# One layer of a streaming step on one core: where the search part transposes a tile's picks, and where the mixers run the next unit's head

## The reference

```python
u = rmsnorm(h, g_mix);  z = u @ w_in
zq, zf, zi, zg, zx, zy = split(z)
# A: four heads, in chunks of 64 tokens; f = lb + (1 - lb) * sigmoid(zf), k = 1 - f, q = silu(zq)
S_t = diag(f_t) S_{t-1} + k_t^T i_t ;  o_t = S_t^T q_t
oA = rmsnorm(o) * silu(zg)
# B: width-4 causal conv of zx, two block-diagonal gates r and i, then a scan
a = exp(-8 * r * softplus(-lam));  b = sqrt(1 - a^2) * (i * xc);  h_t = a_t h_{t-1} + b_t
oB = h * gelu(zy)
h += concat(oA, oB) @ w_out
h += peer(rmsnorm(h, g_ffn))
h += (p @ w_ple) * sigmoid(rmsnorm(h, g_ple) @ w_ple_gate);  y = rmsnorm(h, g_final)

def peer(x):                      # 8 heads, top 16 of 128 x 128 experts, 16384 in all
    q = x @ w_q;  s = q . keys    # two halves a head
    pick the 16 best sums of the two halves' top 16;  g = softmax(those sums)
    return sum_k g_k * gelu(U[e_k] . x) * V[e_k]
```

## Time and profile before

| | us |
|---|---|
| median of 3 runs | 3629.16 (3627.43 to 3629.78) |
| the profiled execution | 3632.48, its span 3630.8 |
| mixers | from about 350 to 610 |
| search part, six rounds over the tiles | from about 1140 to 1612 |
| TensorE busy | 3233.1, 89% of the span |
| VectorE busy | 2724.1, 75% |
| ScalarE busy | 1060.8, 29% |
| GpSimd busy | 975.9, 27% |
| mean granted TensorE clock | 0.941 of full speed |

### The profile page before, as it was taken

How to read it: one execution, slowest core, us unless ns; L and a number is a source line. 1 busy time by engine, 2 the same in 40 slices (tenths; PEclk the granted TensorE clock), 3 DMA queues, 4 the chain that set the end, 5 groups by cost and what they waited for, 6 DMA issues and landing times. The chain is left out here.

```text
span 3630.8 us, 52472 instructions
## 1 busy us (share of the span) xinstructions
PE 3233.1 (89%) x17880; PEld 2942.6 (81%) x17880; DVE 2724.1 (75%) x4967; ACT 1060.8 (29%) x1419; POOL 975.9 (27%) x796
## 2 busy tenths in 40 slices
PE   6998566979979999899999987779999999999988
PEld 6998344779979988899999987768888888888778
DVE  3000766268889888889999987659999999999853
ACT  3112434121122222225555531122222222222233
POOL 0000000000002444444444446423333333333300
PEclk9999666989989999999999999889999999999989
DMA  3223221011145888889999999889999999999721
GB/s 112 86 86 108 79 76 61 18 28 39 26 125 181 253 263 252 246 252 306 323 326 324 323 332 338 298 292 352 359 352 354 359 353 350 351 357 345 248 76 53
DMA packets 411350, 822.83 MB, mean 227 GB/s; under 512 B 40704, under 2 KB 262800, under 8 KB 403856
## 3 DMA queue, kind: packets, MB, share of 16 engines
q1 hardware_dynamic: 300688, 419.27, 35.4%
q0 software_dynamic: 110592, 402.70, 32.6%
HBM read 696.74 MB, written 125.12 MB: 226 GB/s over the span
## 5 line engine op out<-in xcount | busy, mean ns | idle before, releaser
L232 PE MATMUL ea_pa<-rest_hi,ea_uhi 128*128 128x384 f32 x2048 | 711.5, 347 | 131.5 <-DVE ea_ulo L1415 129.8
L1137 POOL DMA_INDIRECT h<-in_peer_u,ga_rows x384 | 562.6, 1465 | 741.6 <-DVE ea_acc L1542 513.1
L233 PE MATMUL ea_pa<-rest_lo,ea_uhi 128*128 128x384 f32 x2048 | 698.3, 341 | 0.0
L234 PE MATMUL ea_pa<-rest_hi,ea_ulo 128*128 128x384 f32 x2048 | 698.2, 341 | 0.0
L1137 POOL DMA_INDIRECT eo_ring<-in_peer_v,ga_rows x384 | 406.3, 1058 | 695.7 <-DVE h L1826 629.1
L232 PEld LDWEIGHTS ea_pa<-rest_hi,ea_uhi 128*128 128x128 f32 x2048 | 395.5, 193 | 143.8 <-issue 93.1
L1826 DVE SCALAR_TENSOR_TENSOR h<-eo_ring,eo_share,h 128x1024 f32<-128x1024 f32 x384 | 490.9, 1279 | 0.5 <-DMA eo_ring<-in_peer_v,ga_rows 0.5
L1542 DVE CUSTOM_DVE_ANT_0 h<-h,plain 128x1024 f32<-128x1024 f32 x384 | 454.2, 1218 | 42.0 <-DMA h<-in_peer_u,ga_rows 41.9
L233 PEld LDWEIGHTS ea_pa<-rest_lo,ea_uhi 128*128 128x128 f32 x2048 | 395.6, 193 | 0.0
L234 PEld LDWEIGHTS ea_pa<-rest_hi,ea_ulo 128*128 128x128 f32 x2048 | 394.8, 193 | 0.0
L1762 ACT ACTIVATE eo_phi<-eo_prod 128x512 fp32r<-128x512 f32 x192 | 121.6, 633 | 775.7 <-DVE eo_prod L1800 724.2
(11 more groups left out here) (317 smaller groups left out, 6203.5 us busy)
## 6 DMA issues: line engine op xcount, KB each, us to landing
ea_raw<-in_peer_u SPq DMA_DIRECT2D x512, 128.0 KB, 5.7
region<-in_peer_v SPq DMA_DIRECT2D x128, 512.0 KB, 10.4
act_scratch<-ea_stage SPq DMA_DIRECT2D x128, 384.0 KB, 4.9
w_scratch<-region SPq DMA_DIRECT2D x24, 2048.0 KB, 12.0
region<-w_scratch SPq DMA_DIRECT2D x16, 1536.0 KB
region<-act_scratch SPq DMA_DIRECT2D x16, 1536.0 KB
eo_wt<-w_scratch SPq DMA_DIRECT2D x16, 1536.0 KB, 13.7
eo_at<-act_scratch SPq DMA_DIRECT2D x16, 1536.0 KB, 18.0
```

The source lines that it names most:

```text
L232: nc.tensor.matmul(out, w[0], x[0], start=first, stop=False)
L233: nc.tensor.matmul(out, w[0], x[1], start=False, stop=False)
L234: return nc.tensor.matmul(out, w[1], x[0], start=False, stop=last)
L1137: nc.gpsimd.indirect_dma_start(out=dst, out_offset=None, in_=table, in_offset=bass.IndirectOffsetOnAxis(ap=self.rows[:, m % GT, m // GT:m ...
```

## The change

In the search part TensorE's three transposes of a tile's picks stand behind the fifth of the eight blocks instead of the eighth, and ScalarE's three copies of them stand in its seventh step, behind that step's `hi`, instead of behind the eighth. VectorE's queue is as before.

In the mixers the loops are written out. The head of a unit (VectorE: L671 to L695; ScalarE: the three sigmoids and Ln; TensorE: the transpose of the state rows) stands ahead of the tail of the unit before: on VectorE behind the copies that signal `oc_ready`, on ScalarE behind Sqrt (L650) and ahead of Square, on TensorE behind the chunk products of the samples. For that q, x, the conv result and the parameters have two buffers, q and x are loaded two units ahead (the second unit's at the start), the old rows are copied out of PSUM first, Square writes to r and Gelu to ig, and a few semaphores are new. The diff, cut to its core:

```diff
@@ mixers: the loads at the start, on SP
                 for load in (load_f, load_x, load_v, load_q, load_g, load_s, load_y):
                     load(e, 0)
+                load_x(e, 1)
+                load_q(e, 1)
@@ mixers: SP, in a unit
                         e.wait_ge(o_sum, i + 1)
-                        load_q(e, i + 1)
+                        if i + 2 < 4:
+                            load_q(e, i + 2)
                         load_s(e, i + 1)
                         e.wait_ge(oc_ready, i + 1)
-                        load_x(e, i + 1)
+                        if i + 2 < 4:
+                            load_x(e, i + 2)
@@ mixers: ScalarE
-                with e.Fori(0, 4) as i:
-                    e.wait_ge(all_used, i + 1)
+                def head(i):
                     e.wait_ge(in_f, (i + 1) * 16)
+                    if i > 0:
+                        e.wait_ge(sf_used, i)
                     f(sf[:], zf[:], ACT.Sigmoid).then_inc(sig_f, 1)
...
+                    e.wait_ge(f_ready, i + 1)
+                    f(cum[:], sf[:], ACT.Ln).then_inc(ln_f, 1)
+
+                head(0)
+                for i in range(4):
+                    cur = cur_two[:, i % 2]
                     e.wait_ge(v_t, i + 1)
                     f(vtok[:], ps_v, ACT.Copy).then_inc(v_tok, 1)
-                    e.wait_ge(f_ready, i + 1)
-                    f(cum[:], sf[:], ACT.Ln).then_inc(ln_f, 1)
                     e.wait_ge(cum_ready, i + 1)
...
                     f(sf[:], sf[:], ACT.Sqrt).then_inc(sqrt_b, 1)
+                    if i + 1 < 4:
+                        head(i + 1)
                     e.wait_ge(o_sum, i + 1)
-                    f(cum[:].rearrange("p (t c) -> p t c", c=128), ps_o, ACT.Square).then_inc(o_sq, 1)
+                    e.wait_ge(oc_ready, i + 1)
+                    f(r[:].rearrange("p (t c) -> p t c", c=128), ps_o, ACT.Square).then_inc(o_sq, 1)
                     e.wait_ge(ms_ready, i + 1)
                     f(rs[:], rs[:], ACT.Sqrt).then_inc(rms_root, 1)
                     e.wait_ge(in_y, (i + 1) * 16)
-                    f(sq[:], zy[:], ACT.Gelu_apprx_tanh).then_inc(gelu_y, 1)
+                    f(ig[:], zy[:], ACT.Gelu_apprx_tanh).then_inc(gelu_y, 1)
@@ mixers: VectorE
                     e.wait_ge(state_t, i + 1)
-                    e.wait_ge(in_x, (i + 1) * 32)
-                    link(v.tensor_copy(xs[:, :, 0:3], ps_state[:, 0:24].rearrange("p (b j) -> p b j", j=3)))
+                    e.wait_ge(in_x[i % 2], (i // 2 + 1) * 32)
+                    v.tensor_copy(old[:, i % 2], ps_state[:, 0:32]).then_inc(old_ready, 1)
+                    e.wait_ge(old_ready, i + 1)
+                    link(v.tensor_copy(xs[:, :, 0:3], old[:, i % 2, 0:24].rearrange("p (b j) -> p b j", j=3)))
...
+                head(0)
+                for i in range(4):
+                    main(i)
+                    if i + 1 < 4:
+                        head(i + 1)
+                    tail(i)
@@ mixers: TensorE
-                with e.Fori(0, 4) as i:
+                def state_rows(i):
+                    e.wait_ge(in_rows, (i + 1) * 32)
+                    e.wait_ge(all_used, max(i, 1))
+                    tr(ps_state, rows_in[:], P.ident[:]).then_inc(state_t, 1)
+
+                state_rows(0)
+                for i in range(4):
                     e.wait_ge(all_used, i + 1)
-                    e.wait_ge(in_rows, (i + 1) * 32)
-                    tr(ps_state, rows_in[:], P.ident[:]).then_inc(state_t, 1)
                     e.wait_ge(in_v, (i + 1) * 16)
...
                     last.then_inc(dss_ready, 1)
+                    if i + 1 < 4:
+                        state_rows(i + 1)
                     e.wait_ge(st_ready, i + 1)
...
                     e.wait_ge(oc_ready, i + 1)
+                    e.wait_ge(old_ready, min(i + 2, 4))
                     tr(ps_rows, cols_out[:], P.ident[:]).then_inc(oc_t, 1)
@@ experts: ScalarE  (T_STEP = 4)
                     quad(i * Q_DENSE + GT, lambda r: exponentials(i + GT) if r == 2 else None)
-                    quad(i * Q_DENSE + (GT + 1))
-                    e.wait_ge(rows_t, i + 1)
-                    cols = bass.ds(i * 128, 128)
-                    for x, scale in ((0, 1.0), (1, 1.0), (2, G_SCALE)):
-                        nc.scalar.activation(picks[:, x, cols], pr[:, x], ACT.Copy, scale=scale).then_inc(picks_hi, 1)
+                    quad(i * Q_DENSE + (GT + 1), lambda r: copy_picks(i) if r == T_STEP + 2 - 4 else None)
@@ experts: TensorE
-                    quad(i * Q_DENSE + GT)
-                    quad(i * Q_DENSE + (GT + 1))
-                    e.wait_ge(rows_ready, i + 1)
-                    for n in range(3):
-                        last = nc.tensor.transpose(pr[:, n], rows[:, n], P.ident[:])
-                    last.then_inc(rows_t, 1)
+                    for r in range(4 * Q_DENSE):
+                        for n in range(ND_N):
+                            product(*at_block(i * Q_DENSE + GT, r + 1), n)
+                        if r == T_STEP:
+                            e.wait_ge(rows_ready, i + 1)
+                            for x in range(3):
+                                last = nc.tensor.transpose(pr[:, x], rows[:, x], P.ident[:])
+                            last.then_inc(rows_t, 1)
```

More of the change, by code:

```diff
@@ L564, in mixers @@
          st_ready, sn_ready, att_sum, att_ready, qdz_ready, o_sum, o_sq, ms_ready, rms_root, on_ready, on_t,
-         state_t, xc_ready, silu_g, gates, va_ready, sqrt_b, gelu_y, oc_ready, oc_t, rows_ready, self_ok) = (s(n) for n in (
+         state_t, old_ready, sf_used, e3_used, xc_ready, silu_g, gates, va_ready, sqrt_b, gelu_y, oc_ready, oc_t, rows_ready, self_ok) = (s(n) for n in (
              "stored", "cur", "used", "sig_f", "sig_q", "sig_g", "sig_r", "sig_i", "f", "ln_f", "cum", "dl",
@@ L568, in mixers @@
              "st", "sn", "att_sum", "att", "qdz", "o_sum", "o_sq", "ms", "rms_root", "on", "on_t",
-             "state_t", "xc", "silu_g", "gates", "va", "sqrt_b", "gelu_y", "oc", "oc_t", "rows", "self"))
+             "state_t", "old", "sf_used", "e3_used", "xc", "silu_g", "gates", "va", "sqrt_b", "gelu_y", "oc", "oc_t", "rows", "self"))
         NSTORE = 6
@@ L612, in _ @@
                 load_wg(e, 0)
-                with e.Fori(0, 3) as i:
-                    unit(i, True)
-                unit(3, False)
+                for i in range(4):
+                    unit(i, i < 3)
                 e.wait_ge(stored, 5 * NSTORE * 16)
@@ L697, in _, with main @@
                     e.wait_ge(xc_ready, i + 1)
+                def main(i):
+                    zq, xc, xp, xs, cur = (x[:, i % 2] for x in (zq_two, xc_two, xp_two, xs_two, cur_two))
                     e.wait_ge(ln_f, i + 1)
@@ L770, in _, with tail @@
                     v.tensor_copy(cols_out[:, 28:36], by(xc[:, SAMPLE], DS)[:, :, DS - 1]).then_inc(oc_ready, 1)
+                def tail(i):
+                    zq, xc, xp, xs, cur = (x[:, i % 2] for x in (zq_two, xc_two, xp_two, xs_two, cur_two))
                     e.wait_ge(o_sq, i + 1)
-                    link(v.tensor_reduce(rs[:], cum[:].rearrange("p (t c) -> p t c", c=128), AX.X, ALU.add))
+                    link(v.tensor_reduce(rs[:], r[:].rearrange("p (t c) -> p t c", c=128), AX.X, ALU.add))
                     v.tensor_scalar(rs[:], rs[:], 1.0 / 128, EPS, ALU.mult, ALU.add).then_inc(ms_ready, 1)
@@ L793, in _ @@
                 mm, tr = nc.tensor.matmul, nc.tensor.transpose
-                with e.Fori(0, 4) as i:
+                def state_rows(i):
[3 more added lines that the diff above has]
+                state_rows(0)
+                for i in range(4):
+                    zq, xc = zq_two[:, i % 2], xc_two[:, i % 2]
                     e.wait_ge(all_used, i + 1)
-                    e.wait_ge(in_rows, (i + 1) * 32)
-                    tr(ps_state, rows_in[:], P.ident[:]).then_inc(state_t, 1)
                     e.wait_ge(in_v, (i + 1) * 16)
@@ L1367, in exponentials, with copy_picks @@
                     nc.scalar.activation(rows[:, 2], rows[:, 2], ACT.Exp).then_inc(exped, 1)
+                def copy_picks(i):
+                    e.wait_ge(rows_t, i + 1)
+                    cols = bass.ds(i * 128, 128)
+                    for x, scale in ((0, 1.0), (1, 1.0), (2, G_SCALE)):
+                        nc.scalar.activation(picks[:, x, cols], pr[:, x], ACT.Copy, scale=scale).then_inc(picks_hi, 1)
                 hi(0, 0)
```

82 lines of the change are left out of this document (45 added, 37 removed).

## The result

The changed kernel takes 3548.27 us (3545.12 to 3549.67) beside 3628.81 for the kernel before: a ratio of 0.9777, 95% interval 0.976 to 0.9794. Run again later, it was 3553.32 beside 3626.43, ratio 0.9802 (0.9785 to 0.9818). So 80.5 and 73.1 us less; forecast were 75.9. The profiled execution took 3547.42 us; the one of before, 3632.48, lay above its median, so the two traces differ by 85.1.

What follows compares the result with a forecast made beforehand. VectorE's waits were taken to bound the search part (last step on the picks) and the mixers (norm's sum, then the next head). Savings of 54.3 + 21.6 = 75.9 us gave a median of 3553 us, range 3541 to 3580.

Steps and rivals of the forecast that it cites:

- Middle boundaries: Dense search part, between tiles: VectorE's first five waits at the last step on the picks vanish, giving back 44.8 us.
- Last boundary: End of the dense search part, no following tile: 9.5 us back, between TensorE's 8.3 and VectorE's 13.67.
- Gathers at no cost: Dense search part: the same gathered bytes in less time, 285 GB/s at DMA share 0.95, costing nothing.
- Rival 4: Dense search part: VectorE waits for gathered rows, costing 157 us, total 3710 us; chance 4%.
- The head fits: Mixers: the next unit's head, 8.6 us on VectorE, fits the 8.64 to 9.4 us gap between scan and norm.
- Rival 2: Mixers: the moved head makes Square late and the norm slips, losing the 24.9 us gain, total 3578 us; chance 6%.
- The added table load is covered: Mixers, before the norm's root: ScalarE's extra 1.28 us load fits in its 1.63 us idle stretch, costing nothing.
- The mixers' pace: Mixers: moving the head three times saves 8.3 us each, 24.9 us in all, bounds 24.9 and 27.6.
- Up to attention: Mixers, from the turn of the units: attention products start at 11.7 us instead of 19.98, 8.3 us a unit.
- later than 12 us: Mixers: attention starting more than 12 us after the turn of the units would show the forecast wrong.
- nothing changes: Mixers, behind the start of attention: the rest of each unit takes as long as before, no gain or loss.
- The start: Start of the mixers: three added loads, 1.18 MB at 354 GB/s, delay the first state rows by 3.3 us.

Runs made afterwards that it cites:

- the two runs with all fillers: Changed kernel, state rows ahead of most loads, identity transposes ahead of v's transposes, gates, attention and output products: 3529.57 us; with q, g also ahead of rows: 3526.43 us.

## Why the prediction was right, point by point

**Middle boundaries: right.** Five were to give back 44.8 us. From the first turn to the sixth, before took 393.23 us (1147.17 to 1540.40) and the changed kernel 347.88 (1119.97 to 1467.85): 45.35. The rounds take 69.4 to 70.0 us (69.6). The slack of the copies is 7.9 us (7), and the run one block later shows what it hangs on. VectorE bounds, as the working had it. TensorE's wait for the softmax cost nothing that shows.

**Last boundary: the reason right, the size 2.6 us too large.** I took 9.5 us, between TensorE's 8.3 and VectorE's 13.67. The dense part became shorter by 55.7 in the mean of the table's rows with and without the search change, so 10.4 fall to this boundary; the weighted part became 3.5 longer. In its first pair of copies, 45.1 us apart instead of 43.6, VectorE now waits for the split behind TensorE's blocks, as the rows at 1540.70 and 1552.04 show. Over the whole weighted part these waits are 4.3 us in the first trace of the changed kernel, 1.2 in the second and 3.6 in the search part alone, where it is 5.8, 2.4 and 4.0 us longer than 501.1: most of it. Two of the later ones in the first trace (1815.80 and 1904.36) come behind waits of ScalarE for a store of the weights (6.0 us until 1810.69, 6.7 until 1899.27); the second trace has no such later wait of VectorE. Net 6.9, below my lower end of 8.3: I had not counted what VectorE loses behind the boundary. The search part as a whole gives 52.2 by the traces (54.3 predicted, bounds 49.8 and 58.5) and 55.9 by the medians of the run with it alone.

**Gathers at no cost: right.** 286 GB/s at 0.94 stand where 285 and 0.95 were worked out, and VectorE waits 0.5 us for gathered rows in the dense part. Rival 4 did not come.

**The head fits: right.** The norm's sum waits 0.24 and 0.31 us behind the moved head in the second and third units and nothing in the first. Rival 2 did not come.

**The added table load is covered: right.** It runs from 472.12 to 473.40 while VectorE sums, and the root starts at 473.80, when VectorE's L800 has ended. The Trainium skill (ScalarE: Activation LUTs, What ACT_TABLE_LOAD costs) adds a drain of some 1380 ns to a load. By that rule the trace disagrees here too: the load starts as Square ends, and the root starts 0.40 us after the load's end.

**The mixers' pace: two steps mis-sized, in opposite directions.** I worked out 24.9 us, with an upper bound of 27.6. From the first scan to the output projection it was 241.8 us in the mean of the three traces with the old mixers and 213.0 in the five with the new: 28.8, above the bound. The units came 50.2 to 51.7 us apart, two of fifteen 53.5; some 53 was expected of all. The means of the pieces say where.

*Up to attention: less than worked out.* I had attention 11.7 us after the turn of the units, and "later than 12 us" was named as a sign of being wrong. The sign came: 12.0, 12.5 and 12.7 us in the first trace, 13.1 three times in the second. The step that failed is the 1.38 us from the gates to attention. I had ScalarE's table load done at 9.4, ahead of the gates' end; but ScalarE stands at the wait for the gates first and loads behind it (438.61), so it is 2.76 us in every moved unit. Where the gates took less than the 6.85 of the earlier trace rows, as the 5.64 above, that hid a part of it. Up to attention 22.4 us came back, not 24.9.

*From attention on: "nothing changes" was wrong by 6.4 us.* The attention products themselves are 3.5 us shorter over four units, by TensorE's clock: in units two to four of the five traces 13 of 15 took 2.25 us, in the old mixers one of nine. I had taken their row from the earlier trace rows at 0.50 and left it there. The other 2.9 us lie behind them: the norm's sum comes 1.0 us sooner behind the last of the four small copies, the tail is 1.3 shorter, and 0.6 lies between attention and those copies. The runs don't explain these three.

Why the level was mostly the upper one is open too. The changed kernel's shorter pauses (2.76 instead of 3.70 us ahead of attention, 1.31 instead of 7.05 ahead of the gates) go with it, but units with the same pauses came out differently, and with pauses of 1.4 to 2.0 us, in the two runs with all fillers, two of six still had 3.9 us.

**The start: about right in size, not quite in its reason.** 3.3 us were worked out from 1.18 MB at 354 GB/s. The rows came 3.3 us later and the first scan 3.4 to 4.9. The run with the loads moved back recovers all of it. But the trace of the changed kernel has the rows themselves issued later, at 362.45 instead of 358.57, since SP issues the three loads from 358.02 to 361.99 and the next block starts behind them. From issue to the transposes the rows took 6.8 us, before 7.4. So the delay is one of issuing, and the bytes give nearly the same figure. Before, then after:

```profile
358.57 0.38 SPq L517 DMA_DIRECT2D mx_rows_in<-in_state_conv  x1
```

```profile
359.12 2.87 SPq L493 DMA_DIRECT2D mx_zq<-z_scratch  x1
362.45 0.38 SPq L520 DMA_DIRECT2D mx_rows_in<-in_state_conv  x1
```

Whether this long issue of 2.87 us is itself a wait for the bytes ahead isn't shown. They do count: with only f and x ahead, the rows took 1.9 us from issue to the transposes (358.11 to 360.04).

**The sum: in part luck.** 52.2 from the search part and 28.8 − 3.8 from the mixers (3.8 is how much later the first scan came, in the mean of the same traces) make 77.2, between the two medians' 73.1 and 80.5. The errors (search part 2 less, mixers 3.4 more, and within the mixers 2.5 less and 6.4 more) lie on opposite sides, so the total came out nearer than its terms. The 85.1 of the two profiled executions contain 7 us of spread.

## What to carry to other kernels

A wait that ends at another engine's queue is moved by moving the work ahead in that queue, and the check is a table of when each block ends on each engine: it gave the slack of 7 us here, and one block later the wait was back. An engine's idle stretch can take work of the next round if that work depends on nothing the stretch waits for; count it step by step against the gap, and look at what the added loads stand ahead of. Where an engine loads a table for a step, see whether the load stands ahead of the step's wait or behind it: here it was behind, and cost 1.28 us on the path of each moved unit. And the duration of a matmul read from a trace holds only for the granted clock of that row, so one row of 4.18 us could not tell what the same products take after the change.

## What the runs showed of the hardware

**The same matmuls at two speeds in the same mixers.** Eighteen attention products took 4.18 us at 0.50 and 2.25 at 1.00, in the same place of the same mixers, behind pauses of the same 2.76 us. In two traces of the unaltered kernel before, those of the first unit took 3.61 and 4.18 us. The Trainium skill (TensorE: Matmul & The Clock Gate, What's actually happening) says that the point at which the clock changes differs from run to run of one kernel; these traces agree.

**The output products ran long at the lower level.** They stayed at 0.50 for 8.00 us in which TensorE counted as busy in all 8.00. With transposes in the pause ahead the clock was at 1.00 when they began, and the same products took 6.3 us instead of 10.8 (456.55 to 467.37 in the changed kernel).

**A filled pause moves.** Gates 2.7 us faster made the pause behind them 2.7 us longer, and the loss came one step later. Fillers paid in the trace where the products behind them bounded the unit (the last unit, 53.8 us instead of 59.3), and where the pauses around the turn were filled together (output projection at 575.6 instead of 583.7).
